# Gate and up weights of an expert in two transfers of 2 MB or four of 1 MB

## The reference

```
a, b = jnp.split(xi @ w_gu[e], 2, axis=-1)     # w_gu[e]: 1024 x 1024, gate | up
return (jax.nn.silu(a) * b) @ w_down[e]        # w_down[e]: 512 x 1024
```

## Time and profile before

| what | us |
|---|---|
| median of 3 runs | 889.68 (887.58 to 890.31) |
| the profiled execution, its own time | 888.9 |
| its span in the profile | 887.2 |
| TensorE (PE) busy | 744.4, 84% of the span |
| TensorE's weight load (PEld) busy | 384.7 |
| VectorE (DVE) busy | 217.6 |
| ScalarE (ACT) busy | 138.1 |
| GpSimd (POOL) busy | 187.4 |
| bytes moved | 247.55 MB, mean 279 GB/s |

### The profile page before, as it was taken

How to read it: one execution, slowest core, us unless ns; L and a number is a source line. 1 busy time by engine, 2 the same in 40 slices (tenths; PEclk the granted TensorE clock), 3 DMA queues, 4 the chain that set the end, 5 groups by cost and what they waited for, 6 DMA issues and landing times.

```text
span 887.2 us, 10055 instructions
## 1 busy us (share of the span) xinstructions
PE 744.4 (84%) x3636; PEld 384.7 (43%) x3636; DVE 217.6 (25%) x546; ACT 138.1 (16%) x338; POOL 187.4 (21%) x186
## 2 busy tenths in 40 slices
PE   3999999979898999829999997878777787787883
PEld 3788688857666645523333332222222222222220
DVE  4331104266749332271111011001010010100110
ACT  4212413013253411101000000000000000000000
POOL 6010000160300000012233332321312313223121
PEclk9999999989997999958999999999999999999998
DMA  9742823020420194477999999999999999999992
GB/s 313 115 148 60 262 106 104 1 72 1 182 106 0 43 425 186 153 277 292 408 409 407 413 410 405 415 407 416 411 411 415 409 413 416 408 416 411 413 417 85
DMA packets 75812, 247.55 MB, mean 279 GB/s; under 512 B 24656, under 2 KB 43999, under 8 KB 51163
## 3 DMA queue, kind: packets, MB, share of 16 engines
q1 hardware_dynamic: 62625, 232.00, 66.2%
q0 software_dynamic: 11776, 8.58, 4.4%
q10 hardware_dynamic: 1378, 6.54, 1.8%
HBM read 240.99 MB, written 24.92 MB: 300 GB/s over the span
## 4 chain that ended last, share of the span: by engine, by line
PE 40%; SPq 29%; DMA 14%; DVE 11%; issue 3%; ACT 2%; POOL 0%; ACTq 0%; DVEq 0%; POOLq 0%
PE bank L1063 37%; SPq L570 20%; SPq L577 9%; DMA reg_b<-in_exp_w_gu 6%; PE bank L1066 3%; DMA reg_a<-in_exp_w_gu 3%; DMA reg_w<-in_exp_w_gu 3%; DMA reg_x<-in_x_prompt 1%; DVE reg_a L1722 1%; DVE reg_y L1973 1%; DVE reg_a L1802 1%; DVE reg_a L1712 1%; DVE reg_x L1712 0%; DVE small L1763 0%; POOL small L673 0%
## 5 line engine op out<-in xcount | busy, mean ns | idle before, releaser
L1063 PE MATMUL bank<-reg_w,reg_y 128*64 128x512 f32 (+2 forms) x512 | 136.8, 585 | 18.4 <-DMA reg_w<-in_exp_w_gu 18.4
L1063 PE MATMUL bank<-reg_a,reg_y 128*64 128x512 f32 x528 | 124.5, 607 | 22.7 <-DMA reg_a<-in_exp_w_gu 16.8
L1063 PE MATMUL bank<-reg_b,reg_y 128*64 128x512 f32 x528 | 123.4, 600 | 22.5 <-DMA reg_b<-in_exp_w_gu 16.8
L1977 DVE TENSOR_TENSOR reg_y<-reg_y,bank 128x256 f32<-128x256 f32 x32 | 13.5, 421 | 418.9 <-ACT reg_y L1046 418.9
L1063 PEld LDWEIGHTS bank<-reg_w,reg_y 128*64 128x64 f32 (+2 forms) x512 | 46.1, 146 | 103.5 <-issue 59.5
L1063 PE MATMUL bank<-reg_b,reg_w 128*128 128x260 f32 x384 | 85.3, 383 | 0.0
L1063 PEld LDWEIGHTS bank<-reg_a,reg_y 128*64 128x64 f32 x528 | 34.3, 138 | 104.2 <-issue 50.5
L1063 PEld LDWEIGHTS bank<-reg_b,reg_y 128*64 128x64 f32 x528 | 34.4, 136 | 102.4 <-issue 56.9
L1063 PEld LDWEIGHTS bank<-reg_b,reg_w 128*128 128x128 f32 x384 | 72.7, 190 | 12.0 <-issue 1.1
L673 POOL TENSOR_TENSOR small<-small 128x1 f32<-128x1 f32 (+4 forms) x18 | 20.2, 1127 | 197.2 <-DVE small L1855 68.1
L739 POOL DMA_INDIRECT out_y_p<-reg_y,reg_q x16 | 25.3, 1582 | 166.5 <-ACT reg_y L1050 166.5
(11 more groups left out here) (341 smaller groups left out, 657.1 us busy)
## 6 DMA issues: line engine op xcount, KB each, us to landing
reg_a<-in_exp_w_gu SPq DMA_DIRECT2D x44, 1024.0 KB, 27.9
reg_b<-in_exp_w_gu SPq DMA_DIRECT2D x44, 1024.0 KB, 28.7
reg_w<-in_exp_w_gu SPq DMA_DIRECT2D x40, 1024.0 KB, 27.9
reg_a<-in_exp_w_down SPq DMA_DIRECT2D x22, 1024.0 KB, 28.4
reg_b<-in_exp_w_down SPq DMA_DIRECT2D x22, 1024.0 KB, 28.1
reg_h<-in_exp_w_down SPq DMA_DIRECT2D x20, 1024.0 KB, 28.3
reg_w<-in_w_in SPq DMA_DIRECT2D x9, 1024.0 KB, 10.6
reg_w<-in_w_out SPq DMA_DIRECT2D x1, 4096.0 KB, 13.3
```

Source lines behind the costliest of these rows:

```text
L1063: return eng.matmul(out, lhsT, rhs, start=start, stop=stop, skip_group_check=True)
L1977: tt(hid[b], silu[b], bank[2 + b][:, 256:512], ALU.mult).then_inc(S["hid_made"], 1)
```

## The change

`GU_PARTS` goes from 4 to 2. The gate and up weights of an expert are then loaded by two transfers of 4 chunks (2 MB, 16 KB a partition) instead of four of 2 chunks (1 MB, 8 KB a partition). With the constant the semaphores change too: TensorE waits ahead of chunks 0 and 4 instead of 0, 2, 4 and 6, and it frees the buffer behind chunks 3 and 7 instead of 1, 3, 5 and 7. The down weights, the buffers, the order and the sum of bytes stay.

```
-GU_PARTS = 4
+GU_PARTS = 2
```

## The result

| | before | after |
|---|---|---|
| median, us | 889.61 (887.58 to 890.31, 4 runs) | 911.73 (908.88 to 913.88, 4 runs) |
| profiled execution, own time, us | 888.9 | 908.88 |
| its span, us | 887.2 | 907.1 |
| mean granted clock of TensorE | 0.962 | 0.92 |

The ratio is 1.0251, 95% interval [1.0215, 1.0286]. I had forecast 889.5 and a range of 886.3 to 893.5, so the result lies far outside.

A forecast was written before the change was run, and what follows sets the result against it. The DMA stream of weights was taken to bound the kernel; start +1.7, end +1.7 and rate -3.6 us summed to -0.2 us, giving a median of 889.5 us, with an 8-in-10 range of 886.3 to 893.5.

The forecast's parts named there:

- The bound: From the first refill on, time is the DMA stream's start, its bytes over its rate, and what follows the last landing.
- Start, +1.7: Start of the weight stream: first part freed 8 matmul instructions later, first refill issued at 406.04 instead of 404.32, +1.7 us.
- End, +1.7: After the last gate-up landing of expert 31: 16 matmul instructions (3.68 us) instead of 8 (1.96 us), +1.7 us.
- Rate, -3.6: Weight stream of 29 experts: fewer packets and completion writes save 0.125 us an expert, -3.6 us, bounds 2.2 to 5.4.
- my three terms: Stream start +1.7, end +1.7 and rate -3.6 us, summing to -0.2 us.
- The later frees and longer waits cost nothing: Inside the stream: 28 us of DMA queue hides later frees, TensorE's idle fifth hides its lumpier start; no cost.
- The rival of the scatters: Expert stage: small packets wait behind 16 KB ones, landings go from 8.7 to 14.7 us, scatters bound; 917 us, chance 0.04.
- a limit of 13.6: Chain of scatters from expert to expert: the second scatter's landing decides the time only from 13.6 us on.
- The clock: TensorE in the expert stage: a granted clock under 1.00, from longer waits at a stretch, would make the forecast wrong.

The follow-up runs named there:

- coarse waits with small transfers: Changed kernel, but each of its two parts is loaded by two 1 MB transfers with 8 KB rows, waits and frees staying those of two parts: 893.17 us, ratio 1.0041.
- 8 KB rows in big transfers: Changed kernel, but each 2 MB transfer has two 8 KB rows a partition, chunks taken in the order 0 1 4 5 2 3 6 7: 892.87 us, ratio 1.0039.
- split waits: Changed kernel, but scatters to out_y_p and out_y_s have their own semaphores, each waiting only for the previous expert's scatter to the same output: 888.47 us, ratio 0.9987.
- the run with 4 KB rows: Kernel before, with each of its four parts loaded by two transfers of one chunk, waits and frees unchanged: 897.69 us, ratio 1.0089.

## Why the prediction was wrong, point by point

**The bound.** Right for the kernel before. Wrong for the one after: the loads don't set its end, the chain of scatters and gathers does.

**Start, +1.7.** Right. In the kernel before the first refill was issued 404.32 - 400.57 = 3.75 us after TensorE's first instruction; after, by the timeline,

```profile
405.57 3.77 SPq L570 DMA_DIRECT2D reg_a<-in_exp_w_gu  x2
```

with TensorE's first at 400.09, so 5.48: 1.73 more.

**End, +1.7.** Right as a mechanism (3.68 us for 16 instructions in the runs with coarse waits). Start and end together were to cost 3.4; coarse waits with small transfers cost 893.17 - 889.47 = 3.7.

**Rate, -3.6.** Right, with the size of a packet's share a little small. The part that packets have in it was 29 x 107 ns = 3.1 us. From 8 KB rows in big transfers (892.87) to split waits with 16 KB rows (888.47) it is 4.4 us, and the last landing moves from 868.3 to 864.5 us. Per packet that is 3.8 us / (29 x 16) = 8.2 ns, where I had 6.7 between bounds of 3.6 and 10.5. Records of the load queue fell by 62625 - 53409 = 9,216, which is 8,192 packets and 16 x 64 completion writes. The sum of my three terms, -0.2, with bounds of -2.3 and +1.2, comes out in the kernel with split waits, which shows -1.0.

**The later frees and longer waits cost nothing.** Right in itself: coarse waits cost no more than start and end.

**The rival of the scatters.** This is the step that failed. I had its mechanism, gave it 0.04 and a price of 917, and dismissed it by "a burst lies largely where down weights pass, which keep 8 KB packets", hence 10 to 12 us and a limit of 13.6. Two things were wrong in it. The limit came from the period of 16.0 us in the middle of the stage. But the first ten experts run at 12.5 us, and there the limit is 12.5 - 1.9 - 0.5 = 10.1 us (9.7 with 0.86 us from a landing to the next issue, as from 447.51 to 448.37 in the kernel after): above the 9.0 to 9.3 of before, but at the very bottom of the 10 to 12 that I expected myself. By my own numbers the chain would in all likelihood become the bound from the first steps on. And the place of the burst is no constant: it was read from one burst in the middle of the stage. Already the first bursts of the changed kernel lie on gate-up weights, as the window at 425 to 428 us shows, before TensorE is late at all, and so do most of those of the run with 4 KB rows in its first ten steps. With out_y_s landing in 13 us the chain has 1.9 + 13.0 + some 0.8 = 15.7 us, some 3 more than TensorE takes, and the lead is gone.

The doubled landing was a little overdone (14.7 us expected in the worst case; 13.0 in the median, 14.8 at most), and so was my count of 25 experts at 1.1 us: the loss comes all in the first ten steps (37 us), nothing is lost after them, and 13.5 us come back at the end. That 917 lies near the measured 911.7 is luck.

**The clock.** I named a lower grant as a way to be wrong. It fell, to 0.90 at 600 to 700 us of the kernel after. But TensorE waits for its tokens there, so this is an effect and not the cause, and it adds little: in the chain from 440 to 560 us, where the lead is lost, TensorE has 2.2%.

```profile
by line: DMA reg_y<-ffn_in,reg_q 55.4%; DMA out_y_s<-reg_h,reg_q 35.0%; issue 7.6%; POOL out_y_s L739 6.5%; PE bank L1066 2.2%; POOL out_y_p L739 0.8%; POOLq L739 0.1%; POOLq L752 0.1%; POOLq L734 0.1%; POOLq L756 0.0%
```

The same line shows the gather with more than the scatters: it stands in the same queue behind them and lands as late (12.7 to 13.8 us in this chain). That the wait for the scatters is what binds is shown by the run with split waits, which changes this wait alone.

## What to carry to other kernels

A longer row in a bulk load is cheaper for the load and dearer for whatever shares the engines with it: before making packets longer, look up the landing times of the small transfers and the shortest time in which the code that waits for them comes round, not its mean. Where a stage begins with buffers full, the pace of its first steps is worth as much as its bound later on: a chain slower than that pace eats the lead, even if it is no slower than the loads. And a chain of small transfers is often cut by a finer wait: here one semaphore for each output turned 2.5% slower into 0.1% faster.

## What the runs showed of the hardware beyond that

- Two transfers of 64 neighbouring partitions in place of one of 128 brought the stream to 229 to 236 GB/s with all engines at a share of 1.02; with even and odd partitions it kept 415. So it is not the number of rows in a transfer that is slow, but which rows they are. Whether that lies with the partitions or with the rows' places in memory, which change along with them, no run here tells.
- A load of 1 MB took 27.9 us to land in the kernel before, one of 2 MB took 13 to 15 in the changed kernel, where SyncE waits for free buffers instead of for the queue (an issue takes 0.33 us there, 2.08 before), and some 40 with split waits, as more bytes then stand in the queue.
- TensorE was granted 1.00 while busy for 76 to 80 us of 100 with waits of up to 2.0 us for weights, and 0.90 while busy for 82 of 100 with waits of up to 5.3 us for tokens (4.3 with even and odd partitions, 0.90 too). A higher busy share did not bring the higher clock; part of it is the lower clock itself, at which the same instructions take longer. In the kernel after, a wait of 4.28 us ended at 450.54 us; the granted clock was 0.61 from 451 to 452, 0.50 until 458, and 16 matmul instructions took 6.48 us instead of 3.65. A long wait is not the only way to a fall: with split waits, after waits of 1.63 and 2.04 us with 3.65 us of work between them, the clock was 0.63 from 834 to 838 us.
